# Latent attention on one Trainium2 core: projection pieces and last transposes ahead of the next head's scores, and their copy ahead of all four exponentials

## The reference, cut to what matters

```python
def mla_mixer(h, k_nope, k_rope, v, cos, sin, w_in, g_q, w_uq, w_out):
    cq, gate = jnp.split(h @ w_in, [Q_LORA], axis=-1)
    q = (rms_norm(cq, g_q) @ w_uq).reshape(Bsz, S, MLA_HEADS, QK_NOPE + QK_ROPE)
    q_nope, q_rope = jnp.split(q, [QK_NOPE], axis=-1)
    q_rope = apply_rope(q_rope, cos[:, :, None, :], sin[:, :, None, :])
    o = causal_block_attention(q_nope, q_rope, k_nope, k_rope, v)   # blocks of 128 queries
    o = o.reshape(Bsz, S, MLA_HEADS * V_HEAD) * jax.nn.silu(gate)
    return o @ w_out
```

## Time and profile before

| What | Value |
|---|---|
| median of three runs | 1761.55 us (1761.37 to 1764.08) |
| the profiled execution's own time | 1762.64 us |
| its span | 1760.8 us |
| TensorE busy | 1702.6 us, 97% of the span |
| ScalarE busy | 842.5 us, 48% |
| VectorE busy | 1019.3 us, 58% |
| POOL busy | 705.5 us, 40% |
| granted TensorE clock, mean | 0.996 of full speed |

### The profile page before, as it was taken

The page is one execution under the profiler, slowest core; times in us unless marked ns, Lnnn a source line. Parts: engine busy times, 40 slices in busy tenths (PEclk is TensorE's granted clock), DMA queues, the critical chain, the costliest instruction groups (busy, mean ns, idle before and its releaser), DMA issues.

```text
span 1760.8 us, 24655 instructions
## 1 busy us (share of the span) xinstructions
PE 1702.6 (97%) x8729; PEld 1384.4 (79%) x8729; DVE 1019.3 (58%) x1600; ACT 842.5 (48%) x1472; POOL 705.5 (40%) x795
## 2 busy tenths in 40 slices
PE   9999999979999999999989999999999999999998
PEld 6877777756786667878878888888888888888887
DVE  6677685678457864376658657766624443232322
ACT  5465665876366654356542354465523332323131
POOL 2634445415442015311124423234245555555554
PEclk9999999999999999999999999999999999999999
DMA  7362624322321003201048521111133323333333
GB/s 221 109 198 77 189 74 121 97 71 72 86 88 39 25 13 87 60 25 37 25 152 257 177 61 37 49 48 49 48 96 96 96 73 99 97 103 96 96 96 108
DMA packets 217151, 160.55 MB, mean 91 GB/s; under 512 B 8334, under 2 KB 190615, under 8 KB 217047
## 3 DMA queue, kind: packets, MB, share of 16 engines
q1 hardware_dynamic: 201758, 125.50, 24.8%
q10 hardware_dynamic: 15288, 33.66, 5.8%
HBM read 156.98 MB, written 2.16 MB: 90 GB/s over the span
## 4 chain that ended last, share of the span: by engine, by line
PE 64%; issue 12%; DVE 9%; ACT 8%; POOL 7%; DMA 1%; POOLq 0%; DVEq 0%; ACTq 0%; SPq 0%
PE ps L658 14%; PE ps L662 14%; PE ps L659 13%; POOL wl L608 7%; PE ps L3147 3%; PE ps L3150 3%; PE ps L3148 3%; PE ps L2206 2%; PE ps L2188 1%; ACT wh L621 1%; PE ps L1653 1%; PE ps L1621 1%; PE ps L2195 1%; PE ps L2711 1%; PE ps L2745 1%
## 5 line engine op out<-in xcount | busy, mean ns | idle before, releaser
L608 POOL TENSOR_TENSOR wl<-raw,wh 128x256 fp32r<-128x256 f32 (+1 forms) x775 | 682.1, 910 | 995.7 <-ACT wh L621 995.7
L658 PE MATMUL ps<-ah,wh 128*128 128x512 f32 (+1 forms) x1144 | 458.1, 400 | 12.5 <-ACT gate_u L2784 4.2
L662 PE MATMUL ps<-ah,wl 128*128 128x512 f32 (+1 forms) x1144 | 447.3, 391 | 0.2
L659 PE MATMUL ps<-al,wh 128*128 128x512 f32 (+1 forms) x1144 | 446.5, 390 | 0.0
L621 ACT ACTIVATE wh<-raw 128x1024 fp32r<-128x1024 f32 (+1 forms) x220 | 230.7, 1049 | 300.9 <-PE ps L662 155.4
L658 PEld LDWEIGHTS ps<-ah,wh 128*128 128x128 f32 (+1 forms) x1144 | 213.9, 187 | 67.6 <-ACT wh L621 9.8
L662 PEld LDWEIGHTS ps<-ah,wl 128*128 128x128 f32 (+1 forms) x1144 | 213.9, 187 | 49.5 <-POOL wl L608 1.9
L659 PEld LDWEIGHTS ps<-al,wh 128*128 128x128 f32 (+1 forms) x1144 | 214.1, 187 | 43.8 <-issue 1.7
L658 PE MATMUL ps<-bh,wh 128*128 128x512 f32 (+1 forms) x332 | 134.7, 406 | 9.6 <-DVE resid L1478 3.6
L662 PE MATMUL ps<-bh,wl 128*128 128x512 f32 (+1 forms) x332 | 131.1, 395 | 0.8 <-POOL wl L608 0.7
L659 PE MATMUL ps<-bl,wh 128*128 128x512 f32 (+1 forms) x332 | 130.5, 393 | 0.0
(11 more groups left out here) (451 smaller groups left out, 2966.6 us busy)
## 6 DMA issues: line engine op xcount, KB each, us to landing
raw<-w_mlp SPq DMA_DIRECT2D x64, 512.0 KB, 3.9
raw<-w_in SPq DMA_DIRECT2D x52, 512.0 KB, 3.8
raw<-ssm_w_in SPq DMA_DIRECT2D x40, 512.0 KB, 3.9
ada_late<-w_ada ACTq DMA_DIRECT2D x16, 1024.0 KB, 6.5
ada_raw<-w_ada ACTq DMA_DIRECT2D x16, 512.0 KB, 4.5
cum_rows<-cum_saved ACTq DMA_DIRECT2D x16, 512.0 KB, 3.9
raw<-ssm_w_out SPq DMA_DIRECT2D x16, 512.0 KB, 3.4
raw<-mla_w_in SPq DMA_DIRECT2D x11, 512.0 KB, 4.0
```

The lines of the kernel that those rows point to most:

```text
L608: nc.gpsimd.tensor_tensor(wl[:, s, part], raw[:, s, part], wh[:, s, part].bitcast(F32), ALU.subtract).then_inc(lo_ready, LOW_PIECES * (par ...
L658: nc.tensor.matmul(dst, w_hi[k], x_hi[k], start=k == 0, stop=False)
L659: nc.tensor.matmul(dst, w_hi[k], x_lo[k], start=False, stop=False)
L662: ins = nc.tensor.matmul(dst, w_lo[k], x_hi[k], start=False, stop=k == n - 1)
```

## The change

On TensorE the projection pieces and early output pieces move to the top of a head, then come the last transposes of the head before, then the scores of the next head. On ScalarE the copy of those last transposes moves from between the second and the third exponential to ahead of all four.

```diff
@@ pe_mla @@
             for h in range(MH):
-                if h + 1 < MH:
-                    scores(h + 1)
-                if h:
-                    turn_probs(h - 1, 2)
                 if h // QUAD + 1 < QUADS:
                     for piece, ks in Q_PARTS[h % QUAD]:
                         project_q(h // QUAD + 1, piece, ks)
                 out_pieces(OUT_EARLY.get(h, ()))
+                if h:
+                    turn_probs(h - 1, 2)
+                if h + 1 < MH:
+                    scores(h + 1)
                 if h % 2 == 0 and h:
                     outputs(h // 2 - 1)
                 turn_probs(h, 0)
@@ act_mla @@
             for h in range(MH):
-                if h + 1 < MH:
-                    exp(h + 1, 0)
-                    exp(h + 1, 1)
                 if h:
                     copy_turned(h - 1, 2)
                 if h + 1 < MH:
-                    exp(h + 1, 2)
-                    exp(h + 1, 3)
+                    for t in range(TT):
+                        exp(h + 1, t)
```

## The result

| | before | changed |
|---|---|---|
| median of five runs | 1761.55 us (1761.34 to 1764.08) | 1770.3 us (1769.13 to 1772.04) |
| ratio | | 1.0044, 95% interval 1.0031 to 1.0057 |
| profiled execution, its own time | 1762.64 us | 1769.13 us |
| its span | 1760.8 us | 1767.3 us |
| S(0) to the last output product, profiled | 113.15 us | 120.75 us |

The change makes the kernel slower, by 7.8 us of its ratio (0.0044 x 1761.55; 5.5 to 10.0 by the interval) and 8.75 us between the medians. Forecast were 4.4. The profiled execution of the changed kernel is the fastest of its five.

A forecast was written before the change was run, and what follows sets the result against it. TensorE, busy 97%, bounds the kernel, idling 9.7 us in the head loop. Intervals, each the longer of ScalarE's and TensorE's sides, end the loop at 654.91 against 650.50: 1761.55 + 4.4 = 1766.0 us, range 1760.8 to 1772.0.

The forecast's parts named there:

- No gain to speak of from the waits before scores: Head loop: TensorE's waits before scores total only 1.9 us; the sum by the gap-filling rule would be 1759.7 us.
- The first head: First head: projection stands ahead of S(1), the scores of head 1, and waits for bank 0; S(1) starts 3.75 us late.
- The link through C0 and T2: Next scores wait for last transposes (T2), which need the first copy (C0), queued behind exponentials; link adds 1.08 us.
- The fourth heads: Heads 3, 7, 11: ScalarE's queue makes the interval 8.23 us (first 8.44); the 2.2 us bank 0 standstill lies inside.
- Exponentials 4.3 us after the scores: Each head, ScalarE: without the copy in between, the four exponentials end 4.30 us after the scores began.
- The clock: Loop: sum assumes full clock; rival has it fall at 2.2 us standstills, 6 us in all, 1772, chance 0.12.
- The stages behind move by as much: Behind the head loop: TensorE bounds the later stages, which keep their distance, so the end also moves 4.4 us.
- The rivals of no change and of a gain: Loop: link shorter than its rows, 1763.9 us, chance 0.16; projection fills gaps and link hides, 1756.6 us, chance 0.08.

The follow-up runs named there:

- the filler: Changed kernel plus eight small unread matmuls into free bank 1 ahead of the projections of heads 4, 8 and 12: 1767.66 us, ratio 1.0021 to the kernel before.
- the single and the joint edits: Changed kernel with the first copy ahead of the fourth exponential, with projection banks 0 and 1 alternating, or with both: ratios 1.0019, 1.004, 0.9962 to the kernel before.
- the two edits together: Changed kernel with the first copy ahead of the fourth exponential and projection pieces alternating between banks 0 and 1: 1757.28 us, ratio 0.9962 to the kernel before.
- C0 early: Changed kernel with ScalarE's first copy ahead of the fourth exponential in odd heads and head 0: 1766.41 us, ratio 1.0019 to the kernel before.
- banks in turn: Changed kernel with the twelve projection pieces put into banks 0 and 1 alternately: 1769.73 us, ratio 1.004 to the kernel before.
- the transposes first: Kernel before with only the last transposes and their copy moved as in the change, projections staying behind the scores: 1776.99 us, ratio 1.0077.
- the projections first: Kernel before with only projections and early output pieces at the top of a head, scores still ahead of last transposes, ScalarE unchanged: 1776.81 us, ratio 1.0076.
- TensorE's half: Kernel before with only the TensorE part of the change, ScalarE's copy left between second and third exponential: 1775.31 us, ratio 1.0066.

## Why the prediction was right, and where its size was off

- **No gain to speak of from the waits before scores.** Right: they were 1.9 us in the earlier trace rows and are gone in the profile of the changed kernel, and the time rose all the same.
- **The first head.** Right to 0.01 us: 8.51 where 4.75 + 3.75 = 8.50 were forecast, 1.44 of it the wait for bank 0.
- **The link through C0 and T2.** Right: odd heads 5.79 to 5.83, with 5.73 to 5.77 forecast; shown by moving C0 alone, which brings them to 5.04.
- **The fourth heads.** The interval was right at full clock (8.52 and 8.32 with the filler, 8.31 at S(12) in the changed kernel itself; 8.44 and 8.23 forecast), and that the wait for bank 0 lies inside the link's was right too; the single and the joint edits show it.
- **Exponentials 4.3 us after the scores.** Right: behind S(7) at 587.73 the last accumulator read ends at 591.84 + 0.19, 4.30 later, behind S(6) 4.26.

```profile
591.84 0.19 ACT L1776 ACTIVATION_READ_ACCUMULATOR probs<-ps,nmax 128x1 f32 x1
```

- **The clock.** The term that was mis-sized. The sum has zero for it; the rival had 6 us at a chance of 0.12 because the standstill was shorter than the one at 380 us. Behind a standstill of 2.18 us it fell in two of three places of the profiled execution; that cost 2.7 us of the loop. Without it the profiled loop would be 4.9 us over the kernel before; by the filled kernel's runs the loss would be 3.7 us. The measured time lies between forecast and this rival: of the 3.4 us by which the loss exceeds the 4.4 forecast, most is this term. The prediction said that the trace of the kernel before shows one fall, at 380 us. It shows two more, behind the 2.81 us at 919.94 above and behind waits of only 0.50 and 1.23 us around 1113. None came behind the 1.90 us at 350 or the 2.07 at 375. So that trace already showed falls behind longer and shorter waits than 2.2 us, though not behind each, and nothing in it supported a term of zero:

```profile
1111.52 0.38 PE L2665 MATMUL ps<-lr_s,wgs 128*128 128x256 f32 x1 [0.50 <-ACT v_feat L2798]
1113.13 0.47 PE L658 MATMUL ps<-ah,wh 128*128 128x512 f32 x1 [1.23 <-ACT gate_u L2784]
```

```profile
1112.00:1116.00 4.00, 2.87 (x9) 2.28 (x10) 3.97 (x5) 2.30 (x4) 3.51 (x4) 0.75 0.00 0
```

- **The stages behind move by as much.** Right but for draws of the clock: 7.9 us apart behind the wait for `merged` (919.94 before, 927.84 after), 6.5 at the next stage (926.86 and 933.37) and 6.5 at the end.
- **The rivals of no change and of a gain** failed for the reasons given: no exposed interval came out shorter than its sum, and the gain needed ScalarE's side 0.7 and 2.3 us shorter. With the two edits together the odd heads are 0.6 to 0.8 shorter and the fourth ones 2.6 to 2.8, and there is the gain.

What stays open: what decides whether the clock falls behind a standstill, and how often it falls in the executions that weren't profiled. The mean clock of the changed kernel's five runs is 0.992 to 0.995, with the slowest two at 0.994 and 0.992, which fits more falls than the two seen, but no row shows where.

## What to carry to other kernels

In a chain of in-order engines, write down for each piece what must be taken from its bank first, and what stands between that take and the engine's last signal; a move that fills one wait can put the whole queue of another engine on the way to the next piece. Walk such a loop through by row durations, head by head: here that gave each interval of the change to 0.1 us at full clock, though in two of the experiments a link was missed. When two waits are of one length, test their removal together, for neither shows its worth alone.

## What the runs showed of the hardware

- The granted clock fell behind standstills of about 2 us in a loop in which TensorE is otherwise busy (0.57 to 0.66 over the next 4 to 5 us), in some places and not in others with the same work around. In one profiled execution each, it fell behind two of three standstills of 2.13 to 2.18 us in the changed kernel, one of three of 2.16 to 2.20 with C0 early, three of three of 2.39 to 2.60 with banks in turn, one of three of 3.06 to 3.26 and once behind 1.88 with the transposes first. With the projections first (0.78, then 1.48 to 1.52) it fell once in three, with TensorE's half (0.52, then 1.47 to 1.52) never. So the length alone doesn't decide. The wait for `merged` says the same: a fall behind 2.81 us before, none behind 2.84 in the changed kernel. The Trainium skill, "TensorE: Matmul & The Clock Gate", section HAM oscillation, describes such falls in a loop with a wait in each turn, and there in every turn; this trace agrees in kind, with 2 of 3.
- One fall cost 1.2 to 1.7 us here (1.22 and 1.44 in the changed kernel, 1.56 with C0 early, 1.70 with banks in turn, 1.4 behind `merged`).
- Small matmuls nobody reads, 1.95 us of them in each standstill, went with a clock of 1.00 there and a loop 2.7 us shorter.
